# Up projections of a two-block transformer kernel: eight GpSimd sums of turned activations wait until all residual rows are normalised and stored

## The reference

```python
# block 1
h = rms_norm(x, g_pre_mix) * (1 + sc_m) + sh_m
x = x + gt_m * rms_norm(mixers(h @ w_in) @ w_out, g_post_mix)      # S5, Fourier, window attention
h = rms_norm(x, g_pre_ffn) * (1 + sc_f) + sh_f
gate, val = split(dwconv3(h @ w_up))
x = x + gt_f * rms_norm((gelu(gate) * val) @ w_down, g_post_ffn)
# block 2
h = x
h = h + 0.5 * rms_norm(swiglu(rms_norm(h, g1), ffn1_w_gu, ffn1_w_down), g1_post)
h = h + rms_norm(attention(rms_norm(h, ga) @ w_in_2 + b_in_2) @ w_out_2 + b_out_2, ga_post)
h = h + 0.5 * rms_norm(swiglu(rms_norm(h, g2), ffn2_w_gu, ffn2_w_down), g2_post)
out = h + rms_norm(sigmoid(rms_norm(h, gp) @ w_ple_gate) * (p @ w_ple_proj), gp_post)
```

## Time and profile before

| | us |
|---|---|
| median of 3 runs | 3340.12 (3338.78 to 3344.17) |
| profiled execution | 3337.61 |
| its span | 3335.8 |
| PE busy | 3133.6 (94%) |
| DVE busy | 2182.7 (65%) |
| POOL busy | 1689.7 (51%) |
| ACT busy | 1401.2 (42%) |

### The profile page before, as it was taken

How to read it: one execution, slowest core, us unless ns; L and a number is a source line. 1 busy time by engine, 2 the same in 40 slices (tenths; PEclk the granted TensorE clock), 3 DMA queues, 4 the chain that set the end, 5 groups by cost and what they waited for, 6 DMA issues and landing times.

```text
span 3335.8 us, 41479 instructions
## 1 busy us (share of the span) xinstructions
PE 3133.6 (94%) x15015; PEld 2569.6 (77%) x15015; DVE 2182.7 (65%) x2990; ACT 1401.2 (42%) x2651; POOL 1689.7 (51%) x1248
## 2 busy tenths in 40 slices
PE   7978889899999999999999989989998999999988
PEld 4865578678887887788887878878877788878766
DVE  6879772799996224866668861167737766678844
ACT  4135372655543122443334541067714443435532
POOL 3421046666557777545445553344366555445653
PEclk9988999999999999999999999999999999999999
DMA  5534425322333543243346434546351343354433
GB/s 199 124 104 145 129 64 183 133 89 83 117 92 114 212 136 93 88 133 95 108 140 202 128 109 152 180 116 153 97 182 58 114 136 95 113 189 157 142 117 120
DMA packets 338053, 428.47 MB, mean 128 GB/s; under 512 B 62167, under 2 KB 234394, under 8 KB 337092
## 3 DMA queue, kind: packets, MB, share of 16 engines
q1 hardware_dynamic: 261368, 259.81, 26.9%
q10 hardware_dynamic: 71532, 148.90, 12.0%
q0 software_dynamic: 4960, 17.22, 1.6%
HBM read 321.12 MB, written 111.05 MB: 130 GB/s over the span
## 4 chain that ended last, share of the span: by engine, by line
PE 74%; DVE 12%; issue 5%; ACT 4%; DMA 2%; POOL 2%; SPq 1%; ACTq 0%; DVEq 0%; POOLq 0%
PE PS L938 66%; PE PS L2812 3%; PE PS L2829 1%; DVE pt L805 1%; PE PS L2796 1%; PE PS L871 1%; DVE px L808 1%; POOL w_lo L288 1%; DVE dwl L1818 1%; POOL dg_ab L2987 1%; DMA w_raw<-w_out 0%; ACT act L827 0%; PE PS L477 0%; DMA ada<-w_ada 0%; ACT gs__328 L2353 0%
## 5 line engine op out<-in xcount | busy, mean ns | idle before, releaser
L1301 POOL TENSOR_TENSOR sl<-ss,sh 128x512 fp32r<-128x512 f32 x300 | 446.6, 1495 | 537.6 <-ACT sh L1292 537.6
L288 POOL TENSOR_TENSOR w_lo<-w_raw,w_hi 128x512 fp32r<-128x512 f32 (+1 forms) x284 | 411.8, 1481 | 9.6 <-POOL w_hi L284 0.2
L1575 DVE TENSOR_TENSOR cset<-cset,PS 128x512 f32<-128x512 f32 x360 | 236.0, 683 | 264.4 <-PE PS L938 258.3
L938 PE MATMUL PS<-h_hi,sh 128*128 128x512 f32 x960 | 376.5, 392 | 11.9 <-ACT cset L1466 8.6
L284 POOL CAST w_hi<-w_raw 128x2048 fp32r<-128x2048 f32 x71 | 146.2, 2059 | 461.0 <-DMA w_raw<-w_in 191.2
L938 PE MATMUL PS<-h_lo,sh 128*128 128x512 f32 x960 | 376.1, 392 | 0.0
L938 PE MATMUL PS<-h_hi,sl 128*128 128x512 f32 x960 | 375.9, 392 | 0.0
L1784 POOL TENSOR_TENSOR dal<-dar,dah 128x512 fp32r<-128x512 f32 x154 | 236.8, 1547 | 189.0 <-ACT dah L1778 186.4
L1292 ACT ACTIVATE sh<-ss 128x512 fp32r<-128x512 f32 x300 | 189.1, 631 | 331.0 <-DVE ss L1280 319.7
L1280 DVE TENSOR_TENSOR ss<-sr 128x512 f32<-128x512 f32 x300 | 310.7, 1036 | 0.0
L938 PE MATMUL PS<-x_hi,sh 128*128 128x512 f32 x720 | 281.8, 391 | 6.6 <-DVE x_lo L1272 6.0
(11 more groups left out here) (399 smaller groups left out, 7354.9 us busy)
## 6 DMA issues: line engine op xcount, KB each, us to landing
sr<-ffn_w_gu SPq DMA_DIRECT2D x80, 512.0 KB, 5.1
dar<-sd SPq DMA_DIRECT2D x154, 256.0 KB, 2.7
w_raw<-w_down SPq DMA_DIRECT2D x44, 512.0 KB, 4.4
sd<-st_odd ACTq DMA_DIRECT2D x22, 1024.0 KB, 4.5
xs<-px ACTq DMA_DIRECT2D x40, 512.0 KB, 2.9
sr<-w_up SPq DMA_DIRECT2D x40, 512.0 KB, 5.0
w_raw<-w_out SPq DMA_DIRECT2D x32, 512.0 KB, 4.8
w_raw<-w_in SPq DMA_DIRECT2D x28, 512.0 KB, 6.0
```

The lines of the kernel that those rows point to most:

```text
L288: op = e.tensor_tensor(w_lo[b][:, s], w_raw[b][:, s], w_hi[b][:, s].bitcast(F32), ALU.subtract)
L938: mm = e.matmul(o, a[ai], b[bi], start=start and first, stop=stop and end, skip_group_check=shared)
L1301: e.tensor_tensor(s.lo[p][:], src, s.hi[p][:].bitcast(F32), ALU.subtract).then_inc(S("s_op"), 1)
L1575: e.tensor_tensor(out, out, PS[:, b, :], op).then_inc(S("s_ev"), 1)
```

## The change

In `turned_sums_pool` four waits (for the two store semaphores of the residual rows and for the normalised rows of ACT and DVE) move from behind the eight sums of line 1215 to ahead of them. POOL's operations, their order and their operands stay the same.

```diff
             e.wait_ge(S("ht_lo"), 16 * n + 8)
             e.wait_ge(S("ht_f"), 16 * n + 8)
+            for h in range(2):
+                e.wait_ge(S(f"x_st{h}"), 64 * n)
+            e.wait_ge(S("m_xn"), 4 * n + 4)
+            e.wait_ge(S("m_xd"), 4 * n + 4)
             for kh in range(2):
                 hi, lo = h_part(kh, 0)
                 for k in range(4):
                     e.tensor_tensor(x_raw[kh][:, k, :], hi[:, k, :].bitcast(F32), lo[:, k, :].bitcast(F32), ALU.add).then_inc(S("x_p"), 1)
-            for h in range(2):
-                e.wait_ge(S(f"x_st{h}"), 64 * n)
-            e.wait_ge(S("m_xn"), 4 * n + 4)
-            e.wait_ge(S("m_xd"), 4 * n + 4)
             e.wait_ge(S("x_p"), x0 + 8)
```

## The result

The changed kernel takes 3357.05 us (median of 6, 3355.09 to 3360.96) against 3339.62 (median of 6) for the kernel before: 17.4 us more, ratio 1.0049 with a 95% interval of 1.0038 to 1.0060. The forecast was 3360. The profiled execution took 3355.14 us.

A forecast was written before the change was run, and what follows sets the result against it. PE is the bound, its finish in each up projection set by a DVE chain. That chain's lateness, 7.5, 8.0 and 5.7, sums to 21.2 us: 3337.6 + 21.2 = 3358.8, by the median 3361; said 3360, range 3346 to 3369.

The forecast's parts named there:

- Residual rows (1): DVE's last residual rows lose contention with POOL, so POOL's release comes 1.9, 2.0 and 3.9 us earlier at f=0, 1, 2.
- POOL's queue (2): POOL's work from its release to the last x_tmp, with DVE's share: 39.3, 35.9 and 35.9 us at f=0, 1, 2.
- The bound without new pairs: Lower bound: pairing adds nothing to POOL's old queue plus 10.1 us; about -1.6, +3.3, -3.2, a sum of -1.5 us.
- the alternation that the sum was built on: DVE and POOL operations strictly alternate: one DVE sum of 2.2 us, one POOL sum of 1.1, a pair in 3.3 us.
- What is late next (3): DVE from line 1251 to the end of product 3's ss takes 8.5 us; that end is late by 7.5, 8.0, 5.7.
- PE (4): PE idles 5 us or more before product 0 at no cost of its own; DVE's chain ends the wait before product 2.
- a delay of the chain reaches the end whole: In each up projection DVE's chain sets PE's finish, so its lateness, 21.2 us in all, passes fully to the end.
- A: Rival: POOL's queue hides before line 1251 and sl0, keeping the residual rows' 7.8 us gain; 3330 to 3338, chance 0.08.
- B: Rival: only sl0's lateness reaches PE and two later waits absorb it; 2 to 4 us a site, 3347, chance 0.13.
- C: Rival: the new stall before product 0 leaves PE at half clock, unabsorbed; some 2 us a site, 3367, chance 0.12.
- D: Rival: the change does nothing, as the moved waits were already met at 600; ruled out, no chance given.

The follow-up runs named there:

- run 6: Changed kernel with GpSimd's four x_lo[1] subtractions replaced by memsets that read nothing: 3344.93 us against 3340.98 for the kernel before, ratio 1.0010.
- run 2: Kernel before with the four waits moved ahead of the eight sums at f=0 and f=2 only: 3350.69 us against 3340.98, ratio 1.0029.
- run 3: Kernel before, its eight sums waiting only until the residual rows are added up (line 808), four waits still behind them: 3349.30 us against 3340.25, ratio 1.0028.
- run 5: Changed kernel with the eight sums replaced by eight memsets of the same tiles: 3341.78 us against 3340.25 for the kernel before, ratio 1.0001.
- run 1: Kernel before with the four waits moved ahead of the eight sums at f=1 only: 3348.96 us against 3340.25, ratio 1.0024.
- run 7: Kernel before, waits at their old place, GpSimd's cast moved to ScalarE and two x_tmp moved up: 3338.96 us against 3340.98, ratio 0.9994.
- run 8: Kernel before with cast on ScalarE; at f=2 also four sums held behind the waits and x_tmp before x_lo: 3339.95 us against 3340.86, ratio 0.9995.

## Why the prediction was right

**Residual rows (1).** Line 808 shows 1.23 us (said 1.21). POOL's release moved from 11.5 to 9.6 us behind the anchor at f=0 and f=1 and from 13.5 to 9.6 at f=2: 1.9, 1.9 and 3.9, as said.

**POOL's queue (2).** Said 39.3, 35.9 and 35.9 us (its terms add up to 35.8), measured 39.0, 35.5 and 35.5. The step that made the forecast is this: ten us of sums are only a quarter of what stands behind the release, and DVE's sums stand in it too. The bound without new pairs, -1.5 us in all, would have held if POOL and DVE did not share a queue; run 6 shows that they do, by taking four reads out. Nor did POOL's queue run through and leave DVE's operations behind it: DVE's x_raw, ss and x_lo were served between POOL's sums (9.47 us for the four x_lo), which is the alternation that the sum was built on.

**What is late next (3).** From line 1251 to the end of ss 8.3 us, said 8.5. Late by 7.2, 7.5 and 5.3 us, said 7.5, 8.0 and 5.7. Line 1245 took 3.99 us instead of 3.3, because it meets the cast, which is longer than one sum; it came within the same queue.

**PE (4).** The stall before product 0 came (6.69, 5.99, 5.98 us), and it cost nothing of its own. The later waits did not stay as long as said: before product 2 they grew from 2.94, 2.58 and 0.43 us to 4.68, 3.30 and 4.43, before product 6 they went from 3.31, 3.46 and 5.08 to 2.74, 3.44 and 2.73. Product 2 starts 6.5, 7.5 and 5.2 us later, as the chain does (at f=0 0.7 less, since line 1272 of x_lo[2] took 2.28 us there instead of 2.94). The step that was mis-sized is "a delay of the chain reaches the end whole". The forecast was 21.2 us; the chain was late by 20.0, and PE's matmuls slipped by 8.2, 7.5 and 3.2 us at the sites, 18.9; the span grew by 17.5. The -1.1 us in the PE count outside the sites, where both kernels are the same, I take for the drift between two executions. Of the 21.2 us of the sum 17.4 were measured (16.4 by the ratio): 1.2 of what is missing is the chain, about as much is PE's slip against the chain, and the rest is no larger than that drift.

At f=2, 2 us were given back. The stretch behind PE's wait before product 6 there, before and after:

```profile
2599.00:2612.00 13.00, 13.00 (x49) 10.56 (x49) 12.96 (x13) 6.54 (x11) 11.57 (x7) 0.84 0.49 163
```

```profile
2618.80:2632.00 13.20, 13.20 (x58) 10.94 (x59) 13.11 (x13) 7.06 (x13) 12.14 (x7) 1.00 0.60 193
```

The first number behind POOL's is the granted clock, 0.84 against 1.00: a part of the first stretch was run at 1.2 GHz, none of the second, and PE started 49 matmuls in the one and 58 in the other. The wait ahead of it was 5.08 us before and 2.73 after, since the products in front of it had run more slowly behind the longer wait for x_lo (granted clock 0.92 from 2583 to 2599 before, 0.85 from 2602.6 to 2618.8 after). PE's slip at f=2 is 3.2 us both in the changed kernel and in run 2. It is not shown that the shorter wait always gives this back: in run 3 a wait of 2.28 us at the same place was followed by a slow stretch, 12.56 us for 48 matmuls, against 11.00 in the changed kernel and 13.00 before. At f=0 the sign is open: 8.2 us in one trace and 6.6 in the other, for the same 57.0 us of DVE's chain. The 1.6 us between them come behind product 6, where PE's next wait was 0.64 us before, 3.38 in the changed kernel and 1.74 in run 2, and the 12 matmuls behind it took 2.97, 4.58 and 3.00 us.

**The rivals.** A fails: no site is hidden. Its gain of 7.8 us exists (the residual rows are as much faster as it says) but run 5 shows that it is consumed even when the sums are all but gone. B fails: DVE gets past line 1251 where the queue says. C has its stall and its clock (granted 0.71 to 0.73 over the 15 to 16 us behind the stall at the three sites, against 0.89, 0.89 and 1.00 from the same matmul on before), and the wait behind it absorbed both, as the argument against it said: product 2 is no later than the chain. Its price at f=2 even had the other sign. D is excluded by POOL's start at 611.58 instead of 600.68.

## What to carry to other kernels

Where two engines share a resource operation by operation, add both engines' operations into one queue and look at what stands at its end; the slack of one of them by itself (here 5 to 10 us) is not what is free. Holding work back to spare a neighbour pays only if that work does not then lie beside a longer chain of the same neighbour: here 7.8 us were saved on the residual rows and some 28 (20.0 + 7.8) paid on the sums behind them. A count of a stall is not its price: ask which wait comes after it.

## What the runs showed of the hardware

- The pair rule also holds for DVE's normalisation with one SBUF tensor and a column of scalars: 1.42 us for two alone, 3.12 beside POOL's sums (run 3).
- Four idles of PE of nearly the same length before the same 12 transposes at f=0, 3.04, 3.07, 3.06 and 3.04 us (before, run 1, run 7, run 8), were followed by 1.78, 2.82, 1.53 and 2.82 us for them, and one of 2.22 us at f=1 by 2.79 at a granted clock of 0.50 (run 3). So the length of the idle does not by itself tell whether the clock has fallen behind it, and a trace's single site is uncertain by about 2 us for it.
- Eight memsets of 128x512 on GpSimd take 3.80 us, 0.48 each, against 1.26 for a sum of the same size.
